# GpSimd makes each lo-split of a weight tile in two instructions of 512 columns instead of one of 1,024

## The reference

```python
# first block
proj = a @ w_in                       # 1024 -> about 8,800 columns
h = h + merged @ w_out                # attention and state-space branches, merged
h = h + memory_cross_attention(...)   # w_cross_q, w_cross_kv, w_cross_out
h = h + peer_ffn(...)                 # queries; then every token against 128 x 128 experts:
                                      # gelu(x . u_e), gated, times v_e
# second block
proj = rmsnorm(h) @ w_in_2            # mixer with a gated scan and a spatial gate
h = h + mixed @ w_out_2
h = h + (gelu(conv3x3(h @ w_gate)) * (h @ w_value)) @ w_down   # D_FF = 2816
```

## Time and profile before

| | us |
|---|---|
| median of 3 runs | 2028.3 (2027.28 to 2028.88) |
| the profiled execution | 2026.23 |
| its span | 2024.4 |
| PE busy | 1891.2 (93%) |
| DVE busy | 1258.7 (62%) |
| ACT busy | 939.3 (46%) |
| POOL busy | 721.7 (36%) |
| mean granted TensorE clock | 0.972 |

### The profile page before, as it was taken

How to read it: one execution, slowest core, us unless ns; L and a number is a source line. 1 busy time by engine, 2 the same in 40 slices (tenths; PEclk the granted TensorE clock), 3 DMA queues, 4 the chain that set the end, 5 groups by cost and what they waited for, 6 DMA issues and landing times.

```text
span 2024.4 us, 33419 instructions
## 1 busy us (share of the span) xinstructions
PE 1891.2 (93%) x11448; PEld 1597.0 (79%) x11448; DVE 1258.7 (62%) x2214; ACT 939.3 (46%) x1310; POOL 721.7 (36%) x333
## 2 busy tenths in 40 slices
PE   6999887999899989999999999999998899889996
PEld 5998866894766889999999988888856665458885
DVE  2476775630411499367776688888853346569997
ACT  4656624442433534467777433333343532135553
POOL 5887524784333698800000000000004733103332
PEclk9999888999999999999999999999998999899998
DMA  5554302457243366655555866667675432234442
GB/s 186 185 185 166 115 22 73 156 185 254 105 154 125 126 194 219 209 173 177 172 178 170 258 238 239 236 234 237 238 266 180 145 104 84 83 125 170 172 167 82
DMA packets 121684, 343.41 MB, mean 170 GB/s; under 512 B 13776, under 2 KB 46672, under 8 KB 121360
## 3 DMA queue, kind: packets, MB, share of 16 engines
q1 hardware_dynamic: 120096, 335.32, 48.9%
q0 software_dynamic: 1520, 7.21, 1.0%
HBM read 324.65 MB, written 17.83 MB: 169 GB/s over the span
## 4 chain that ended last, share of the span: by engine, by line
PE 52%; DVE 8%; issue 5%; POOL 4%; ACT 1%; DVEq 1%; DMA 0%; POOLq 0%; ACTq 0%
PE banks L854 52%; DVE arena L2365 5%; POOL weight_rest L741 3%; DVE weight_rest L2185 1%; POOL weight_rest L803 1%; ACT weight_high L1390 1%; DVE arena L2378 0%; DMA weight_ring<-in_stream 0%; PE banks L865 0%; ACT arena L1390 0%; DVE act_feature_major L1846 0%; DVEq L2365 0%; DVE act_feature_major L1849 0%; ACT scratch L1390 0%; DVE hidden_high L2379 0%
## 5 line engine op out<-in xcount | busy, mean ns | idle before, releaser
L1390 ACT ACTIVATE weight_high<-weight_ring 128x1024 fp32r<-128x1024 f32 x436 | 460.7, 1057 | 464.6 <-PE banks L854 410.1
L741 POOL TENSOR_TENSOR weight_rest<-weight_ring,weight_high 128x1024 fp32r<-128x1024 f32 x204 | 520.6, 2559 | 238.4 <-ACT weight_high L1390 119.9
L2185 DVE TENSOR_TENSOR weight_rest<-weight_ring,weight_high 128x1024 fp32r<-128x1024 f32 x204 | 250.0, 1225 | 137.9 <-ACT weight_high L1390 135.8
L854 PE MATMUL banks<-a_high,weight_high 128*128 128x256 f32 x1216 | 305.9, 289 | 4.3 <-DVE a_rest L1861 4.1
L854 PE MATMUL banks<-a_rest,weight_high 128*128 128x256 f32 x1216 | 299.8, 284 | 0.0
L1390 ACT ACTIVATE arena<-banks 128x512 f32<-128x512 f32 (+4 forms) x284 | 181.0, 657 | 163.6 <-PE banks L854 161.4
L854 PEld LDWEIGHTS banks<-a_high,weight_high 128*128 128x128 f32 x1216 | 234.3, 193 | 5.0 <-issue 4.5
L854 PEld LDWEIGHTS banks<-a_rest,weight_high 128*128 128x128 f32 x1216 | 234.7, 193 | 0.2 <-issue 0.2
L854 PE MATMUL banks<-weight_high,gated_high 128*128 128x512 f32 x512 | 201.2, 393 | 0.0
L854 PE MATMUL banks<-weight_high,gated_rest 128*128 128x512 f32 x512 | 200.2, 391 | 0.0
L854 PE MATMUL banks<-a_high,weight_rest 128*128 128x256 f32 x1216 | 173.5, 286 | 12.5 <-POOL weight_rest L741 12.5
(11 more groups left out here) (290 smaller groups left out, 3480.3 us busy)
## 6 DMA issues: line engine op xcount, KB each, us to landing
weight_ring<-in_stream SPq DMA_DIRECT2D x504, 512.0 KB, 3.3
arena<-in_stream SPq DMA_DIRECT2D x66, 512.0 KB, 3.2
unit_spill<-small SPq DMA_DIRECT2D x128, 128.0 KB, 3.5
scratch<-unit_spill SPq DMA_DIRECT2D x128, 128.0 KB, 3.2
residual<-in_x SPq DMA_DIRECT2D x2, 512.0 KB, 3.8
arena<-in_mem POOLq DMA_DIRECT2D x2, 512.0 KB, 4.6
arena<-in_ctx POOLq DMA_DIRECT2D x2, 512.0 KB, 5.0
arena<-in_keys POOLq DMA_DIRECT2D x1, 1024.0 KB, 5.1
```

The costliest lines, as they stand in the source:

```text
L741: nc.gpsimd.tensor_tensor(w_lo[:, e % 2, :], raw(e)[0], w_hi[:, e % 2, :], ALU.subtract).then_inc(S["rest_ready"], 1)
L854: return nc.tensor.matmul(out, lhsT, rhs, start=start, stop=stop, skip_group_check=True)
L1390: return nc.scalar.activation(out, in_, f, **kw)
L2185: tt(w_lo[:, e % 2, :], raw(e)[0], w_hi[:, e % 2, :], ALU.subtract).then_inc(S[ready], 1)
```

## The change

Two of GpSimd's helpers make the subtraction for columns 0 to 511 and then for 512 to 1,023. The semaphore is raised by the second. The waits ahead of the first are unchanged; between the two there is none. `in2_rest` (L800) is not in the diff.

```diff
@@ split_rest @@
-                nc.gpsimd.tensor_tensor(w_lo[:, e % 2, :], raw(e)[0], w_hi[:, e % 2, :],
-                                        ALU.subtract).then_inc(S["rest_ready"], 1)
+                for half in (slice(0, 512), slice(512, 1024)):
+                    ins = nc.gpsimd.tensor_tensor(w_lo[:, e % 2, half], raw(e)[0][:, half], w_hi[:, e % 2, half],
+                                                  ALU.subtract)
+                ins.then_inc(S["rest_ready"], 1)
@@ split_down @@
-                nc.gpsimd.tensor_tensor(w_lo[:, e % 2, :], raw(e)[0], w_hi[:, e % 2, :],
-                                        ALU.subtract).then_inc(S["ffn_down_lo_ready"], 1)
+                for half in (slice(0, 512), slice(512, 1024)):
+                    ins = nc.gpsimd.tensor_tensor(w_lo[:, e % 2, half], raw(e)[0][:, half], w_hi[:, e % 2, half],
+                                                  ALU.subtract)
+                ins.then_inc(S["ffn_down_lo_ready"], 1)
```

## The result

The changed kernel takes 2032.87 us (median of 20 runs, 2029.14 to 2037.17), the kernel before 2027.37 (20 runs beside it): ratio 1.002, interval 1.001 to 1.0029. It is slower by 0.1 to 0.3%, by 5.5 us between the medians, where 2.45 us less was forecast; 2032.87 lies 0.2 us outside the range. The profiled execution took 2032.56 us, its span is 2030.8, 6.4 more than before, at nearly the same mean TensorE clock (0.971, before 0.972).

What follows compares the result with a forecast made beforehand. TensorE was taken to set the pace in most stages and VectorE's convolution in the last. The terms +0.4 - 7.8 + 5.55 - 0.6 = -2.45 us took the median from 2028.3 to 2025.9 us, range 2020.5 to 2032.7.

Steps and rivals of the forecast that it cites:

- The last stage: Final stage, 21 turns paced by VectorE's convolution: each turn 0.37 us shorter, -7.8 us in all.
- The interleaving: Last stage: VectorE's waiting step runs between the halves, hiding one step with its gap, 0.35 to 0.37 us a turn.
- the short turn: Last stage: a turn of 8.9 us where it was 9.25, with no convolution step over 1.5 us.
- The turn slips: Rival, last stage: late gate copies let hidden_rest go first, every second turn about 9.35 us; 2030.9 us, chance 0.10.
- The bursts: Stretches of long VectorE operations beside TensorE-bound stages: VectorE's turns inside tiles make TensorE wait, +5.55 us.
- the units: Pattern of 736 to 759 and 800 to 822 us, +4.0 us, and the single pair at 712 to 722, +0.75.
- the peer query: Two 2,048-column VectorE steps at 655 to 664 us, with TensorE's idle before 665.79: +0.8 us.
- The merge: From 365 to 385 us, GpSimd alternating with VectorE's ssd_rest: VectorE done earlier, -0.6 us (0 to -2).
- The open ends: Ends of stages where TensorE waits for the first split, and the last split: some three places, +0.4 us.
- The added instruction: GpSimd's splits: a clean pair of halves ends after 2.50 us, +0.13 us per tile, nearly all under cover.
- No turn between the halves: Rival: the lock passes from half to half, so VectorE gets no turn; 2032.7 us, chance 0.10.

Runs made afterwards that it cites:

- experiment 1: Kernel before with halves only in the last stage's down splits, all other splits whole: 2027.46 against 2027.57 us, ratio 0.9998.
- experiment 8: Kernel before with halved down splits, old copy order, two of four rest matmuls omitted in each down tile but the last: 2024.99 us, one profiled run.
- experiment 2: Kernel before with halves only in the down splits and ScalarE's plain gate copy ahead of the scaled one: 2020.92 us, ratio 0.9968.
- experiment 7: Kernel before with halves in the merge stretch's splits and the down splits, gate copies swapped: 2019.61 against 2026.81 us, ratio 0.9953.
- experiment 4: Kernel before with halves in all splits of L741, the last stage's down splits left whole: 2034.12 us, ratio 1.0027.
- experiment 5: Kernel before with halves only in the splits of the units' loop: 2034.14 against 2026.81 us, ratio 1.0031.
- experiment 6: Kernel before with only the units' splits cut, after 896 columns instead of 512: 2033.09 us, ratio 1.0026.
- experiment 3: Kernel before with the two gate copies swapped and all splits whole: 2027.38 us, ratio 0.9999.

## Why the prediction was wrong, point by point

*The last stage, -7.8 forecast, -1.4 found in the trace* (and -0.1 between the medians of experiment 1). This is the step that failed. The interleaving was right, and the short turn is 8.94 as worked out. Wrong was what is late next: that ScalarE, "which now does its gelu first, can start its gate copies earlier", so that they end 0.25 us earlier. I took the copies of the earlier trace rows to stand behind the gelu. The row just ahead of those says otherwise. Timeline of ScalarE in the kernel before:

```profile
1856.29 0.42 ACT L1390 ACTIVATE arena<-arena 128x256 f32<-128x256 f32 x1 [2.94 <-DVE arena L2365]
1856.89 0.56 ACT L1390 ACTIVATE arena<-banks,cols 128x256 f32<-128x256 f32 x1 [0.17 <-issue]
...
1866.15 0.56 ACT L1390 ACTIVATE arena<-banks,cols 128x256 f32<-128x256 f32 x1 [0.19 <-PE banks L854]
```

The gelu is over at 1856.71 and the copy begins 0.18 later with "issue" as its releaser, which is 0.26 after the gate's bank is full (1855.42 and 1.21 of the earlier trace rows). The same distance to the bank, 0.25, stands after the change and in experiment 8, where the distance to the gelu is 0.43 and 0.18. So it was the bank that set the copies before too, and the same copy one turn later (1866.15) names it as its releaser. Counted from the end of the hidden_high that opens the turn (1848.8 before, 1865.50 after), the bank was full after 7.83 and now after 7.78, and the copies ended after 8.92 and now after 8.88: 0.04 of relief for a turn that is to be 0.3 shorter. With the slip taken away, experiment 2 gains 6.6 of the 7.8. An "issue" of 0.17, where the turn beside it names the bank, was the sign to look for another releaser.

*The turn slips (0.10), 2030.9 forecast.* This rival is what happened: hidden_rest ahead of the first step, every second turn. Its size was off too: I had two waiting steps, 9.35 us; there are three, 9.52, because hidden_rest starts clean, the split behind it comes 0.20 later, waiting for ScalarE's weight copy, and the second step meets its first half. The mean of 9.23 leaves 0.5 of the stage's -1.4 to the turns. The rest, 0.9, lies behind the last turn, where the last four matmuls take 1.08 us instead of 1.91 (rows at the end). Experiments 2 and 7 don't have that gain.

*The bursts, +5.55 forecast, +6.3 found* (640 to 866): +4.75 against 5.7 in the units, +0.8 against 0.6 in the peer query. The mechanism stands, by experiments 4, 5 and 6, though both of VectorE's long operations fell on one tile where I had them on two. But two terms hide in it. TensorE's waits for GpSimd in the units add up to 11.1 us before and to 14.9 after: 3.8 more, a little less than forecast. The other 1.9 is by difference, and two stretches of half clock fall into them.

*The merge, -0.6 forecast, +0.4 found from 322 to 640.* The idle of 2.76 of the earlier trace rows goes away altogether and 4.1 us are gained at once, after 0.9 lost ahead of it: -3.2 from 322 to 390, and the same -3.2 in the traces of experiments 4 and 7. So the place was mis-sized. In the changed kernel's trace the gain is lost again by 640, but not in experiment 4's, whose instructions are the same up to the last stage. The loss comes in some executions (the changed kernel's, experiment 7's) and not in others; experiment 4's profiled one, 2030.56 us, is the second fastest of its twelve. How often it comes isn't shown.

*The open ends, +0.4:* +0.2 at the first matmul and +0.6 at 322, which can't be told from noise: experiment 3, with the same instructions as before up to there, has +1.0. *The added instruction* is right to 0.01. *No turn between the halves (0.10)* is refuted: the halves start at 1866.39 and 1867.77, and VectorE's step of 1866.80 ends at 1868.02, 1.1 us ahead of the second half. The Trainium skill says (SBUF — State Buffer, section "Who interferes with whom") that who issues first has the shared pair for the whole instruction; it says so of VectorE's two-port modes, and that an instruction with two SBUF inputs, as these are, contends as well. The traces agree, if "whole instruction" is taken by the letter: a queued second half doesn't count as issued. Experiment 2 is the gain and experiment 5 the loss from the same fact.

With the slip in place of the full gain and all else as forecast, the sum was +2.65 us (the rival's 2030.9). The span's +6.4 is 3.75 more, as this pair of traces has it: 2.2 in the turns, 1.0 in the merge (with what is lost behind it), 0.75 in the bursts, 0.7 in small shifts (0.2 at the start, 0.1 from 866 to 1800, 0.4 behind the last matmul), less 0.9 at the end, and rounding.

## What to carry to other kernels

Where two engines take turns by whole instructions, as GpSimd and VectorE do here, cutting an instruction of one hands out more turns to the other. It can be a gain where the other engine sets the pace and is a loss where the cut tile is what TensorE waits for, so cut stage by stage and not in the helper that all stages share. And before a gain is booked, follow the next dependence through every engine of the turn down to 0.1 us: here a swap of two ScalarE copies, worth nothing alone, decides whether 6.6 us are there or not.

## What the hardware did that I had not expected

**ScalarE's start after a full bank depends on the instruction.** The copy whose scale and bias come from columns chosen by the loop's counter starts 0.25 us after its bank is full, a plain copy 0.04 after (experiments 2 and 3 against after and 8). Behind the plain copy the scaled one has no such gap; it starts 0.32 after the bank there, so whether the 0.25 counts from the bank or is a cost of going first isn't told apart. That it is the operands picked by the counter that cost this, and not the scaling itself, wasn't tried.

**TensorE's granted clock moves with the waits.** The windows of the kernel after and then of the kernel before, in stretches of the merge, its follow-up and the units (window, length, busy time and count of PE, PEld, DVE, ACT, POOL, granted clock as share of full speed, DMA share, GB/s):

```profile
744.00:752.00 8.00, 7.06 (x46) 7.06 (x47) 7.93 (x3) 2.67 (x4) 7.03 (x5) 0.79 0.56 164
810.00:820.00 10.00, 6.92 (x47) 6.71 (x46) 6.19 (x3) 2.21 (x5) 8.66 (x6) 0.83 0.50 151
...
380.00:395.00 15.00, 15.00 (x118) 14.37 (x117) 4.51 (x6) 7.10 (x9) 15.00 (x12) 1.00 0.54 177
575.00:595.00 20.00, 17.84 (x73) 14.62 (x73) 2.12 (x4) 7.79 (x9) 15.21 (x13) 0.91 0.52 175
```

```profile
744.00:752.00 8.00, 6.75 (x56) 6.54 (x56) 7.91 (x3) 2.96 (x6) 7.51 (x3) 1.00 0.66 201
...
380.00:395.00 15.00, 12.24 (x90) 12.06 (x90) 7.61 (x6) 4.79 (x7) 10.77 (x5) 0.89 0.43 160
575.00:595.00 20.00, 17.80 (x79) 14.50 (x78) 2.67 (x4) 8.39 (x9) 15.24 (x8) 1.00 0.54 184
```

A mean of 0.79 or 0.89 is a part of the window at the lower level, 1.2 GHz, and the rest at 2.4. Before, TensorE had fallen to it in the merge, after its idle of 2.76 us; after, that idle is gone, and so is the fall. In the units two new falls follow the idles of 3.06 and 3.08, and matmuls of 256 columns then start 0.21 us apart instead of 0.12 (experiment 5's rows). Of the two waits of over 3 us near 804 and 813 only the second has the fall behind it, and in experiment 5's trace the first has it (rows at 809.05), so an idle of that length alone doesn't decide it.

In experiment 7's trace the gain of the merge is given back in such falls. Its windows, and those of the kernel before:

```profile
452.00:460.00 8.00, 7.39 (x25) 5.95 (x26) 0.42 (x1) 1.98 (x3) 5.07 (x4) 0.79 0.29 103
505.00:520.00 15.00, 15.00 (x103) 14.82 (x102) 5.10 (x13) 8.80 (x17) 6.00 (x3) 0.77 0.31 102
```

```profile
452.00:460.00 8.00, 5.65 (x31) 4.77 (x31) 1.61 (x4) 2.54 (x3) 4.47 (x3) 1.00 0.32 113
505.00:520.00 15.00, 14.94 (x112) 14.31 (x111) 5.48 (x13) 9.34 (x18) 5.96 (x3) 0.89 0.39 133
```

No instruction of these stretches was changed; they only start 3 us earlier. The shift of the matmuls goes from -3.3 at 390 to 0.0 at 540. The changed kernel gives its gain back as well, part of it in the window of 575 to 595 above (0.91). But in the trace of experiment 4, with the same instructions up to the last stage, that window is at the higher level throughout:

```profile
575.00:595.00 20.00, 19.40 (x86) 16.08 (x87) 1.57 (x3) 7.77 (x8) 17.67 (x14) 1.00 0.63 208
```

So these falls are not the same in every execution of the same code, as the 6.1 and 5.7 us of experiments 5 and 6 at 690 say too. What makes the clock fall there stays open. With it a local gain or loss of some us can't be added up to the end of the kernel, and my sum did so.

At the end of the kernel it goes the other way. TensorE's last four matmuls, in the timeline of the kernel after and then of the kernel before:

```profile
2015.06 1.08 PE L858 MATMUL banks<-weight_rest,hidden_high 128*128 128x512 f32 x4
```

```profile
2008.50 1.91 PE L854 MATMUL banks<-weight_rest,hidden_high 128*128 128x512 f32 x4
```

They run at the higher level after and at the lower before, the idle ahead of the tile being 3.04 us after and 3.51 before. Experiment 1, which has the same ending, gains 1.2 us from the matmul of 2000 on, as the changed kernel does. But experiments 2 and 7 have idles of 3.05 and 3.06 there and run the four matmuls at the lower level (1.91), so the length of the idle doesn't decide this either.
